# A two-layer trunk with a gathered expert layer: front-end weights through the gather ring, a ring of eight slots in place of twelve, eight weight chunks kept

## The reference

```python
def mixer_ab(y, w_in, conv_w, w_out):                       # layer 0
    q, k, v, gate_b, gate_c, h = jnp.split(y @ w_in, 6, axis=-1)
    a_out = stick_breaking_attention(heads(q), heads(k), heads(v))
    b_out = gate_b * causal_depthwise_conv(gate_c * h, conv_w)
    return jnp.concatenate([a_out, b_out], axis=-1) @ w_out

def mixer_conformer(y, ...):                                 # layer 1
    a, g = jnp.split(y @ w_pw1 + b_pw1, 2, axis=-1)
    z = causal_depthwise_conv(a * jax.nn.sigmoid(g), conv_w) + conv_b
    return jax.nn.silu(layernorm(z, ln_g, ln_b)) @ w_pw2 + b_pw2

def peer(y, w_q, sub_keys, u, v):                            # behind each mixer
    q = (yt @ w_q).reshape(T, PEER_HEADS, 2, PEER_HALF)
    val, idx = lax.top_k(jnp.einsum('thpc,pnc->thpn', q, sub_keys), PEER_TOPK)
    cand = val[:, :, 0, :, None] + val[:, :, 1, None, :]
    top_val, top_pos = lax.top_k(cand.reshape(...), PEER_TOPK)
    gate = jax.nn.softmax(top_val, axis=-1)
    act = gate * jax.nn.gelu(jnp.einsum('thkd,td->thk', u[expert], y))
    return jnp.einsum('thk,thkd->td', act, v[expert])
```

## Time and profile before

| | |
|---|---|
| time, three runs | 1648.89, 1650.69, 1652.69 (median 1650.69) |
| the profiled execution's own time | 1650.49 |
| its span from first to last instruction | 1648.7 |
| busy: TensorE, VectorE, ScalarE, GpSimd | 1048.9, 1113.8, 462.7, 503.8 |
| read from memory | 647.48 MB |
| mean granted TensorE clock | 0.788 of full speed |

### The profile page before, as it was taken

One profiled execution on the slowest core, in us unless ns is written; L12 is line 12 of the kernel. 1 busy time (PEld: TensorE's weight loads), 2 busy tenths in 40 slices (PEclk: granted clock), 3 DMA queues, 4 the chain that ended last, 5 costly groups with the idle time before them and its releaser, 6 DMA issues.

```text
span 1648.7 us, 19969 instructions
## 1 busy us (share of the span) xinstructions
PE 1048.9 (64%) x6936; PEld 710.0 (43%) x6936; DVE 1113.8 (68%) x3119; ACT 462.7 (28%) x953; POOL 503.8 (31%) x541
## 2 busy tenths in 40 slices
PE   7896777657744477776685456785766444544444
PEld 7896553434511156655463135664554111111111
DVE  2434658867557765887745766797756777777764
ACT  4101344302111133853221122873221211111110
POOL 0002323433233322332323332333323333333330
PEclk9999877878976689887897579887888655555666
DMA  9819999999999999899999999999999999999995
GB/s 333 328 65 394 418 420 386 421 419 419 417 420 422 421 419 414 348 411 384 417 417 417 422 420 417 371 401 398 411 418 418 422 421 422 421 422 421 419 421 212
DMA packets 105892, 649.84 MB, mean 394 GB/s; under 512 B 11456, under 2 KB 15552, under 8 KB 38208
## 3 DMA queue, kind: packets, MB, share of 16 engines
q0 software_dynamic: 76032, 553.68, 81.3%
q1 hardware_dynamic: 26272, 92.81, 14.5%
q10 hardware_dynamic: 3488, 2.08, 0.4%
HBM read 647.48 MB, written 1.05 MB: 393 GB/s over the span
## 4 chain that ended last, share of the span: by engine, by line
DMA 43%; PE 24%; DVE 16%; issue 5%; ACT 5%; POOL 5%; DVEq 2%; another core or an unknown queue 1%; POOLq 0%; ACTq 0%
DMA ring<-in_uv_dram,expert 31%; DMA wring<-in_wall_dram 12%; PE ps L659 10%; DVE ring L1191 7%; PE ps L842 7%; POOL ring L382 5%; ACT side L560 2%; PE ps L744 2%; DVE side L1246 2%; PE ps L855 1%; PE ps L666 1%; PE ps L883 1%; PE ps L830 1%; DVE picked L1183 1%
## 5 line engine op out<-in xcount | busy, mean ns | idle before, releaser
L1191 DVE CUSTOM_DVE_ANT_0 ring<-ring,ps 128x1024 f32<-128x1024 f32 x528 | 635.2, 1218 | 338.7 <-DMA ring<-in_uv_dram,expert 246.5
L382 POOL DMA_INDIRECT ring<-in_uv_dram,expert x528 | 501.8, 950 | 1110.9 <-PE ps L842 862.8
L842 PE MATMUL ps<-ring,mix 128*32 128x512 f32 x2112 | 366.3, 829 | 306.9 <-DVE mix L1207 303.8
L659 PE MATMUL ps<-yT,wring 128*128 128x128 f32 (+1 forms) x2048 | 279.0, 297 | 95.9 <-DMA wring<-in_wall_dram 58.5
L659 PEld LDWEIGHTS ps<-yT,wring 128*128 128x128 f32 x2048 | 262.9, 203 | 121.6 <-DMA wring<-in_wall_dram 64.8
L842 PEld LDWEIGHTS ps<-ring,mix 128*32 128x32 f32 x2112 | 67.8, 135 | 504.7 <-DVE mix L1207 364.4
L633 ACT ACTIVATE gel<-dots 128x4 f32<-128x4 f32 x132 | 27.1, 205 | 745.3 <-DVE dots L1191 667.6
L855 PE MATMUL ps<-sel,osb 128*128 128x16 f32 x528 | 76.9, 289 | 74.2 <-ACT osb L619 71.1
L855 PEld LDWEIGHTS ps<-sel,osb 128*128 128x128 f32 x528 | 73.6, 223 | 114.5 <-ACT osb L619 110.4
L560 ACT ACTIVATE side<-ident,params 128x128 f32<-128x128 f32 x310 | 97.3, 389 | 17.9 <-PE ps L883 16.3
L830 PE MATMUL ps<-ident,yg 128*128 128x128 f32 x264 | 52.3, 364 | 72.4 <-DVE dots L1191 72.4
(11 more groups left out here) (201 smaller groups left out, 954.4 us busy)
## 6 DMA issues: line engine op xcount, KB each, us to landing
wring<-in_wall_dram SPq DMA_DIRECT2D x160, 512.0 KB
ring<-in_uv_dram,expert POOLq DMA_INDIRECT x528
ring<-in_wall_dram SPq DMA_DIRECT2D x8, 1024.0 KB, 9.7
out_dram<-fo ACTq DMA_DIRECT2D x16, 64.0 KB
hT<-in_xT_dram ACTq DMA_DIRECT2D x1, 576.0 KB, 12.0
hT<-in_xT_dram SPq DMA_DIRECT2D x2, 256.0 KB, 5.0
params<-in_smalls_dram ACTq DMA_DIRECT2D x1, 430.0 KB, 4.4
```

The source lines that it names most:

```text
L382: pool.indirect_dma_start(out=ring[:, i % R, :], out_offset=None, in_=uv, in_offset=bass.IndirectOffsetOnAxis(ap=expert[:, n % 2, k:k + 1] ...
L659: last = pe.matmul(ps[:, m % 2, 0:w], wring[:, i % NB, c, :], rhs(c), start=(c == 0), stop=(c == C - 1))
L842: mm = pe.matmul(po[32 * j:32 * j + 32, half, :], mix[:, k, :], ring[:, slot, D + 512 * half:D + 512 * (half + 1)], start=(q == 0), stop=( ...
L1191: nc.vector.tensor_tensor_reduce(out=row, in0=row, in1=yrep, scale=1.0, scalar=0.0, op0=ALU.mult, op1=ALU.add, accum_out=dots[:, k:k + 1]) ...
```

## The change

- The front end's temporaries move out of the ring into a tile of their own, `kept` (8 x 1024 floats a partition).
- All chunks up to `inB` 15, the 16 of `qA` among them, go through one ring of 20 buffers: the four of `wring` and the 16 halves of the eight ring slots (`BUFFER`). The stream then goes on in `wring` alone.
- R is 8. The first eight gathers wait until the two `inB` chunks in their slot have been multiplied.
- When the temporaries in `kept` are done with, eight `pw1` chunks are loaded there once, and serve both blocks of layer 1.
- 16 `inB` chunks instead of 12 stand ahead of step 0 (`FRONT` -4 to -1), and the four in steps 0's first groups are gone.
- The small parameters are loaded in two parts, the second (conv taps and keys) and the second x block behind ScalarE's squares. ScalarE's `gates(0)` stands behind all of `front` below 0.

```diff
-R = 12
+R = 8
+KEEP = 8
...
-    FRONT = {-3: [("inB", k) for k in range(4)], -2: [("inB", k) for k in range(4, 8)], -1: [("inB", k) for k in range(8, 12)],
-             0: [("inB", 12), ("inB", 13)], 1: [("inB", 14), ("inB", 15)],
-             2: [("inB", 16), ("inB", 17), ("vt", 0), ("vt", 1)],
+    FRONT = {u: [("inB", 16 + 4 * u + k) for k in range(4)] for u in range(-4, 0)}
+    FRONT |= {2: [("inB", 16), ("inB", 17), ("vt", 0), ("vt", 1)],
...
     STREAM = [(k, JOB["inA", k]) for k in range(24)] + [(24 + k, JOB["outA", k]) for k in range(8)]
-    WQ0 = 32
+    STREAM += [(32 + k, JOB["qA", k]) for k in range(16)]
...
+            if (name, k) == ("inB", 16):
+
+                for i in range(KEEP):
+                    for w in range(2):
+                        LOADED[JOB["pw1%d" % w, i]] = len(STREAM)
+                    STREAM.append((48 + i, JOB["pw11", i]))
...
+    EARLY = LOADED[JOB["inB", 15]] + 1
+    BUFFER = [(i - EARLY) % (NB + 2 * R) for i in range(EARLY)] + [NB + 2 * R + i for i in range(KEEP)]
+    BUFFER += [i % NB for i in range(len(STREAM) - len(BUFFER))]
+    BEFORE = [[j for j in range(i) if BUFFER[j] == BUFFER[i]] for i in range(len(STREAM))]
...
-                if i >= NB:
-                    sp.wait_ge(s_proj, STREAM[i - NB][1] + 1)
-                sp.dma_start(wring[:, i % NB, :, :].rearrange("p c n -> p (c n)"), wall[row]).then_inc(s_w[i % NB], 16)
-                if 8 <= i < 24 and i % 2 == 0:
-
-                    j = i // 2 - 4
-                    sp.dma_start(wq0[:, 2 * j:2 * j + 2, :, :].rearrange("p k c n -> p k (c n)"),
-                                 wall[WQ0 + 2 * j:WQ0 + 2 * j + 2].rearrange("k p n -> p k n")).then_inc(s_wq[j], 16)
+                if i == EARLY:
+                    evacuated(sp, "qA", 15)
+                    sp.wait_ge(s_y, 1)
+                if BEFORE[i]:
+                    sp.wait_ge(s_proj, STREAM[BEFORE[i][-1]][1] + 1)
+                sp.dma_start(weights_at(i).rearrange("p c n -> p (c n)"), wall[row]).then_inc(s_w[BUFFER[i]], 16)
...
                     if i >= R:
                         pool.wait_ge(s_vm, i - R + 1)
+                    else:
+
+                        pool.wait_ge(s_proj, JOB["inB", 2 * i + 1] + 1)
...
-            act.dma_start(params[:, :], smalls).then_inc(s_par, 16)
-
-            act.dma_start(hT[:, :, TA:L], xT[:, C * TA:C * L].rearrange("p (c t) -> p c t", t=TB)).then_inc(s_x[2], 16)
+            act.dma_start(params[:, 0:PAR["conv"]], smalls[:, 0:PAR["conv"]]).then_inc(s_par, 16)
...
+            act.dma_start(hT[:, :, TA:L], xT[:, C * TA:C * L].rearrange("p (c t) -> p c t", t=TB)).then_inc(s_x[2], 16)
+            act.dma_start(params[:, PAR["conv"]:NPAR], smalls[:, PAR["conv"]:NPAR]).then_inc(s_par2, 16)
...
-            front(-3)
-            front(-2)
+            for u in range(-4, 0):
+                front(u)
             gates(0)
-            front(-1)
```

More of the change, by code:

```diff
@@ L111, in hybrid_trunk @@
             for k in range(count):
-                LOADED[JOB[name % w, k]] = len(STREAM)
-                STREAM.append((row + k, JOB[name % w, k]))
+                if JOB[name % w, k] not in LOADED:
+                    LOADED[JOB[name % w, k]] = len(STREAM)
+                    STREAM.append((row + k, JOB[name % w, k]))
+    EARLY = LOADED[JOB["inB", 15]] + 1
+    BUFFER = [(i - EARLY) % (NB + 2 * R) for i in range(EARLY)] + [NB + 2 * R + i for i in range(KEEP)]
+    BUFFER += [i % NB for i in range(len(STREAM) - len(BUFFER))]
+    BEFORE = [[j for j in range(i) if BUFFER[j] == BUFFER[i]] for i in range(len(STREAM))]
+    assert all(BUFFER[LOADED[JOB["inB", k]]] == NB + k for k in range(16))
     ctx = ExitStack()
@@ L124, in hybrid_trunk @@
         ring = sb("ring", [P, R, 2 * D])
+        kept = sb("kept", [P, KEEP * D])
         flat = ring[:, :, :].rearrange("p a b -> p (a b)")
@@ L218, in hybrid_trunk @@
         sqB = carve(C, TB)
-        carve, room = carver(flat[:, 0:8 * D])
+        carve, room = carver(kept)
         sq = carve(C, TA)
@@ L251, in hybrid_trunk @@
         s_par = sem("s_par")
-        s_w = [sem(f"s_w{b}") for b in range(NB)]
-        s_wq = [sem(f"s_wq{i}") for i in range(8)]
+        s_w = [sem(f"s_w{b}") for b in range(NB + 2 * R + KEEP)]
+        s_par2 = sem("s_par2")
         s_const = sem("s_const")
@@ L658, in chunk @@
                 for c in range(C):
-                    last = pe.matmul(ps[:, m % 2, 0:w], wring[:, i % NB, c, :], rhs(c), start=(c == 0), stop=(c == C - 1))
+                    last = pe.matmul(ps[:, m % 2, 0:w], weights_at(i)[:, c, :], rhs(c), start=(c == 0), stop=(c == C - 1))
                 last.then_inc(s_proj, 1)
@@ L736, in _ @@
             for k in range(16):
-                m = JOB["qA", k]
-                if k % 2 == 0:
-                    pe.wait_ge(s_wq[k // 2], 16)
                 if k == 0:
                     pe.wait_ge(s_hg2, C)
[L742 to L745, removed]
+                chunk("qA", k, lambda c: hg2[:, c, :], TA)
                 if k == 0:
@@ L906, in side @@
                         chunk("q1%d" % w, k, lambda c: yT[:, c, o0:o0 + P], P)
+            pe.wait_ge(s_par2, 16)
             scores(0)
-            front(-3)
+            front(-4)
             scores(1)
             rows(0)
-            front(-2)
-            front(-1)
+            for u in range(-3, 0):
+                front(u)
             pe.wait_ge(s_sel, 2)
```

13 lines of the change are left out of this document (10 added, 3 removed).

## The result

The changed kernel takes 1817.5 us (median of 4, 1808.3 to 1824.7) where the one before takes 1649.8: a ratio of 1.1015, 95% interval 1.0957 to 1.1073. Measured again (`a_again`) it took 1804.3 us, 1.0937 (1.0916 to 1.0957). So it is slower, as forecast, by 154 to 168 us, where I had forecast 86. The first measurement lies 12 us above the upper end of my range (1655 to 1805), the second at it.

The account below looks back on a forecast made before the run. The prediction took the kernel as DMA-bound by its expert gathers, with TensorE bounding the front end before them. From 1650.5 us, -31.7 + 53 + 48 + 5 + 12 = +86 gave 1736 us, range 1655 to 1805.

Parts of the forecast that it names:

- the ring term: Gather ring cut from twelve slots to eight: each gather waits for values eight back; losses of 53, 48, 5 and 12 us.
- the undisturbed steps: 17.6 steps without side work or many weights: 3.0 us lost a step, 53 us (0 to 95).
- the convolution: Eight steps with layer 1's convolution and norms: 6 us lost each, 48 us (0 to 80).
- the stretches with many weights: Four stretches, some five steps: weight transfers fill holes, 1 us lost each, 5 us (0 to 15).
- the first four steps: Steps from 160 to 320 us: 3 us lost each, 12 us (0 to 22).
- the gain of 31.7 us: Front end and kept chunks: 25 us less DMA work behind the first gather, plus 6.7 us of weight waits gone.
- starves harder: Rival: side-work stalls land fully on the DMA, up to 1830 us; chance 0.16 for above 1790.
- My signs: Steps 25 to 32 at 43 to 45 us, DMA 380 to 400 GB/s, VectorE's gather wait some 350 us, among others.
- Front end: Before the first gather: twelve chunks moved there, eight loads gone, 25 us; 6.7 us of TensorE's weight waits gone.
- The release times: From a group's last gather landing to the issue its values release: 9.04, 10.10, 6.43, 7.82 us for groups 0 to 3.
- The group's transfer: Four gathers issued on an empty queue: first lands after 5.5 us, the others 2.49 us apart, 13.0 us in all.
- The rival "faster": Two groups of slots suffice if empty-queue latency is 4.0 us or less: 1619 to about 1640 us; chance 0.08.

Follow-up runs that it names:

- b_r8: The kernel before the change with gathers going through eight of its twelve ring slots, nothing else changed: 1824.9 us, 1.1056 of the kernel before.
- a_r12: The changed kernel with twelve ring slots instead of eight, temporaries in slots 8 to 11 and no kept chunks: 1627.0 us, 0.9877 of the kernel before.
- m_burst: Gathers alone, no compute, zero output; groups of four issued with 0 to 4 earlier gathers in flight: 14.0 us a group on an empty queue.

## Why the prediction was wrong in size

The direction and the mechanism were right: the ring of two groups of slots starves the DMA, and that is more than the front end gives. The size was not.

The step that failed is the ring term: I had 118 us, and it measured 180 (`b_r8` less before, profiled executions), because a group's transfer was put at 13.0 us where it takes 15.0, and because the steps with weights and the first four were taken as nearly free. Of the 62 us missed, 15 lie in the undisturbed steps, 8 in the convolution, 23 in the stretches with many weights and 17 in the first four steps. The second error is the gain of 31.7 us, of which 7 to 20 came.

By its time the outcome is the rival "starves harder" (above 1790 us, chance 0.16). My signs fell accordingly: a step of 25 to 31 takes 46.4 us and not 43 to 45, the DMA is at 364 GB/s there and not at 380 to 400, VectorE's wait is 483 us and not 350; the side stretches are below 370 GB/s as said (340 and 342). Step by step:

**Front end.** "12; gone: 8; 20 x 1.25 = 25 us" and "6.7 us" of weight waits. The twelve moved chunks and the waits were worked out at 21.7 us and measured at 20.8 where the DMA is the bound (`a_r12`). That the sum fits is in part luck. The twelve chunks are right: `a_r12` has 6.7 MB less of SyncE's transfers behind the first issue (56.6 against 63.3), 15.9 us at 421 GB/s, and of these some 12 us show behind it. The first gather is issued 11.2 us earlier there (11.0 in the changed kernel), not 6.7: the weight waits are gone, the wait for ScalarE is 1.5 us shorter, and the rest I can't name. The eight loads that are gone were put at 10 us, and together with what the kept ones spare behind the first issue they bring 3.5 us with eight slots, which can't be told from nothing. This is the second wrong step, an error of reasoning: I subtracted transfers at the DMA's full rate from a kernel that I had just declared not to be DMA-bound. As I read it, a load that is taken out of a queue with holes leaves a larger hole. (With ten slots, where the queue is nearly full, and four kept chunks the `pw1` stretches are 4.4 and 5.6 us shorter than with twelve and nothing kept; four saved loads are 5.0 us. But nine slots and six kept chunks have 3.9 and 3.5, so this isn't clean.)

**The release times**: 9.04, 10.10, 6.43 and 7.82 us in the forecast, 9.06, 9.49, 6.90 and 7.27 as means of the changed kernel's undisturbed steps. The mean is right (8.35 and 8.18), but the loop that I summed has 10.10 + 7.82 = 17.9 in the forecast and 16.8 measured. So 1.2 us a step of the next error is hidden by this one.

**The group's transfer** is the term that failed: "A group of four then lands 5.5 + 3 x 2.49 = 13.0 us after its first issue". Measured 14.0 on an empty queue (`m_burst`), 14.9 with 4.2 us in it, and 15.0 us as a mean in the changed kernel. With it the loop comes out: 9.49 + 7.27 + 2 x 14.8 = 46.4 us a step. (With eight slots the issue of group g+2 follows the values of group g in every case, so that a step is the sum of two releases and two transfers in the trace by construction; the test of the cause is the table under `m_burst`.) Where I erred about the transfer is the second gather, and the empty queue: the DMA doesn't run empty in the mean, 3.4 us are left, 3.4 + 4 x 2.49 = 13.4 us would do if it stayed full, and the hole makes it 15.0. I had 43.9, that is 3.0 us a step more than the 40.9 of the step I read; the loss is 5.8 in the changed kernel (46.4 against 40.6, steps 25 to 31) and 5.0 in `b_r8`. The upper bound I carried, 46.3, hits this by luck: it was made of a latency of 6.7 us, which is 5.5, and of releases that are too long.
The Trainium skill (DMA: Bandwidth & Descriptors, Anatomy of one DMA) gives an estimate of about 4.4 us for one such transfer by its fit; here one alone lands after 5.5 us, and a chain built on the page's figure would have been further off.

**The other stretches**, `b_r8` less the kernel before, so that the ring is seen alone. Undisturbed steps (4 to 9, 16 to 17, 24 to the end): 20.0 + 3.7 + 46.4 - 2.0 = 68 us, forecast 53. Convolution and norms (11 to 15, 19 to 23): 28.3 + 27.4 = 56 us, forecast 48; 7.0 us a step, forecast 6. Stretches with many weights (9 to 11, 15 to 16, 17 to 19, 23 to 24): 14.2 + 0.1 + 16.5 - 3.0 = 28 us, forecast 5. The first four steps: 28.8 us, forecast 12. Together 180 against 118. "Have weight transfers to fill a hole" failed in the `pw1` stretches; what I had not seen is that there TensorE's four chunks a group stand ahead of the values, so that the slots come back later still. The trace of `b_r8` has this: in the `pw1` stretches TensorE begins a group's values 3.6 and 3.4 us after the coefficients are ready, in undisturbed steps 0.1; from the start of a group's last dot product to the end of its values it is 10.4 and 10.1 us against 7.7. (Before the change it was 12.9 and 12.3 us there, which twelve slots covered.) The group's transfer is longer too, 17.4 and 17.9 us against 14.7. In the first four steps the three numbers are 1.7, 9.2 and 18.2 us. No run moves the chunks behind the values, so how the loss divides between the two isn't shown.

**The sum.** -31.7 + 118 = +86 us in the forecast; +177 for the ring alone (`b_r8`) and 7 to 20 us back for all the rest, as measured. My range's upper end of 1805 left out the case that several terms come near their upper bounds together; since all hang on the same quantity, the queue at the moment of issue, that was to be expected.

**The rival "faster"** needed an empty-queue latency of 4.0 us or less; it is 5.5. The Trainium skill (Trainium Kernel Development and Optimization, Best Practices) says to double-buffer so that DMA and compute overlap; here two groups of slots are not enough for that, and even a ninth slot beyond two groups of four is worth 4.5 us a step.

## What to carry to other kernels

A ring for gathers is sized by time, not by whether it is "double": work out, group by group and not in the mean, the queue that is left when a slot's successor is issued (slots in flight less those waiting for compute), and compare it with what a queue needs to stay full, here between 4.2 and 6.7 us, two to three transfers. Below that each slot taken away costs more than the one before (twelve to ten 2% with the side work, ten to nine 3%, nine to eight 6%), and the bytes that the freed memory saves are worth little (3.5 us of 13.6, not told from nothing), because the DMA now waits. Price gains and losses of one change against the state that the change itself makes.

## What the runs showed of the hardware

- A gather of 1 MiB behind an empty queue lands after 5.5 us, and the next one 3.5 us later though it was issued 1.24 us behind it; from the third on the distance is 2.49 us (`m_burst`, which loads nothing else). In the changed kernel's trace an 8 KB packet takes 0.31 us in a full queue, and 0.58 and 0.39 us on the mean in the two half microseconds from 1530.5 us, where a hole ends.
- A hole comes although gathers are still unlanded: with one gather in flight (landing 1.7 us after the issue) a group loses 2.4 us, about as much as that gather's whole transfer. The landing that a wait sees is the last of 16 increments, and the queue thins out before it: for the gather that lands at 1531.85 us in the changed kernel they come from 1530.42 on, and in the three half microseconds from 1530.0 the DMA moves 279, 262 and 147 GB/s (windows).
